# Scores of differential attention: rounded 128-row products replaced by fp32 products of 32 rows, both maps of a tile issued together

## The reference, cut to what matters

```python
q = _rope(_to_heads(q, 2 * DA_HEADS), pos).reshape(b, DA_HEADS, 2, l, DA_DQK)   # DA_DQK = 32
k = _rope(_to_heads(k, 2 * DA_HEADS), pos).reshape(b, DA_HEADS, 2, l, DA_DQK)
...
s = jnp.einsum('bhcqd,bhckd->bhcqk', qi, k).astype(jnp.float32) * scale
...
p = jax.nn.softmax(jnp.where(mask, s, NEG), axis=-1)
w = (p[:, :, 0] - lam * p[:, :, 1]).astype(v.dtype)
return jnp.einsum('bhqk,bhkv->bhqv', w, v)
```

## Time and profile before

| | us |
|---|---|
| median of 3 runs | 3943.01 (3940.19 to 3950.31) |
| the profiled execution, its own time | 3950.02 |
| its span | 3948.2 |
| PE busy | 3323.5 (84% of the span) |
| DVE busy | 1687.9 (43%) |
| ACT busy | 784.7 (20%) |
| granted TensorE clock, mean | 0.899 |

### The profile page before, as it was taken

How to read it: one execution, slowest core, us unless ns; L and a number is a source line. 1 busy time by engine, 2 the same in 40 slices (tenths; PEclk the granted TensorE clock), 3 DMA queues, 4 the chain that set the end, 5 groups by cost and what they waited for, 6 DMA issues and landing times.

```text
span 3948.2 us, 46980 instructions
## 1 busy us (share of the span) xinstructions
PE 3323.5 (84%) x15268; PEld 2148.3 (54%) x15268; DVE 1687.9 (43%) x2463; ACT 784.7 (20%) x1830; POOL 121.8 (3%) x131
## 2 busy tenths in 40 slices
PE   5999788878796599999769997888787965999994
PEld 3666556656542355555436665566666433555552
DVE  4777524443424122332267775244434241233324
ACT  2222223332211011111122222233322110111111
POOL 2100000000000100000100000000000001000001
PEclk9999997887897799999979998977888977999997
DMA  9400100000100999999820001000001008999996
GB/s 263 137 21 11 38 12 6 6 7 11 43 3 22 355 410 411 410 408 410 313 87 22 21 11 39 12 6 6 7 11 43 3 12 349 414 407 410 409 411 258
DMA packets 141079, 615.53 MB, mean 156 GB/s; under 512 B 13721, under 2 KB 48025, under 8 KB 123033
## 3 DMA queue, kind: packets, MB, share of 16 engines
q1 hardware_dynamic: 104952, 495.89, 31.9%
q0 software_dynamic: 16944, 60.89, 4.8%
q10 hardware_dynamic: 19056, 57.16, 3.9%
HBM read 538.34 MB, written 75.56 MB: 155 GB/s over the span
## 4 chain that ended last, share of the span: by engine, by line
PE 75%; DVE 7%; issue 7%; DMA 5%; ACT 3%; POOL 2%; ACTq 1%; DVEq 1%; SPq 0%; POOLq 0%
PE ps L1080 7%; PE ps L1037 7%; PE ps L1235 6%; PE ps L1336 6%; PE ps L1436 6%; PE ps L1426 6%; PE ps L1395 5%; PE ps L1172 5%; PE ps L1401 5%; PE ps L1453 3%; PE ps L1250 3%; PE ps L1300 3%; DMA arena<-xg 3%; PE ps L1135 3%; PE ps L1160 2%
## 5 line engine op out<-in xcount | busy, mean ns | idle before, releaser
L1172 PE MATMUL ps<-arena 128*64 128x128 f32 (+2 forms) x1440 | 276.3, 331 | 72.4 <-ACT arena L771 40.5
L1080 PE MATMUL ps<-arena 128*128 128x260 f32 x1024 | 294.6, 429 | 34.8 <-DVE rounded L1636 21.1
L1671 DVE TENSOR_REDUCE negmax<-ps 16x1 f32<-16x16 f32 (+8 forms) x216 | 151.5, 705 | 396.1 <-PE ps L1140 395.1
L1037 PE MATMUL ps<-arena 128*128 128x512 f32 (+1 forms) x768 | 259.7, 497 | 5.4 <-DVEq L541 3.2
L1172 PEld LDWEIGHTS ps<-arena 128*64 128x64 f32 (+1 forms) x1440 | 184.1, 163 | 146.5 <-issue 139.7
L1395 PE MATMUL ps<-arena 128*128 128x512 f32 x560 | 254.0, 607 | 2.6 <-ACT arena L959 2.6
L751 ACT ACTIVATE arena<-ps,negmax 16x16 f32<-16x16 f32 (+8 forms) x216 | 151.0, 700 | 519.0 <-DVE negmax L1671 514.8
L1235 PE MATMUL ps<-arena 128*128 128x256 f32 (+1 forms) x1152 | 251.6, 380 | 0.0
L1336 PE MATMUL ps<-arena 128*128 128x512 f32 (+1 forms) x576 | 251.6, 595 | 0.0
L1436 PE MATMUL ps<-arena 128*64 128x256 f32 x2240 | 249.5, 381 | 0.0
L1401 PE MATMUL ps<-arena 128*128 128x256 f32 x1120 | 247.4, 379 | 0.0
(11 more groups left out here) (306 smaller groups left out, 4276.2 us busy)
## 6 DMA issues: line engine op xcount, KB each, us to landing
arena<-w SPq DMA_DIRECT2D x210, 2048.0 KB, 12.9
xg<-arena POOLq DMA_DIRECT2D x51, 512.0 KB, 12.2
arena<-xg ACTq DMA_DIRECT2D x39, 512.0 KB, 10.1
xg<-arena ACTq DMA_DIRECT2D x35, 512.0 KB, 7.6
arena<-w_in SPq DMA_DIRECT2D x16, 1024.0 KB, 5.7
arena<-xg ACTq DMA_DIRECT2D x35, 256.0 KB, 11.2
xg<-arena ACTq DMA_DIRECT2D x70, 128.0 KB, 9.2
arena<-w_in SPq DMA_DIRECT2D x16, 512.0 KB, 4.3
```

Of the source, the lines that this page charges most:

```text
L1037: mm = pe.matmul(dst[0:hi - lo, a:b], w[:, k, lo:hi], uT[:, k, a:b], start=(k == 0), stop=(k == KD - 1))
L1080: mm = pe.matmul(out, w_qk[b][:, k, :], uT[:, k, lo:hi], start=(k == 0), stop=(k == KD - 1), skip_group_check=True)
L1172: mm = pe.matmul(ps[0:AW, 7, at:at + r], V[0:rows(i), i, n * AW:(n + 1) * AW], WT[0:rows(i), g % 3, m * P:m * P + r], start=(i == 0), stop ...
L1671: v.tensor_reduce(negmax[0:r, at:at + 1], flat[0:r, side:side + wide_], AX.X, ALU.max, negate=True)\
```

## The change

Pieces `c` to `f`, their table `sel`, its load and the split into high and low parts are gone. After the rotary the DVE's last addition is made as two of 64 rows, which put q (rows of both maps) and k at the same 64 partitions: `operands_of` gives for a differential head fp32 q and k of 64 rows. Scores are plain fp32 products of 32 rows: map 0 on rows 0 to 31, map 1 on rows 32 to 63. A new function writes both maps of a tile at one point, the start of the step, a product of map 0 and one of map 1 in turn; only tile 8, and the first tile of the forgetting heads, are still written unit by unit. The plans put the remaining pieces `a` and `b` of the next head into steps 8 and 0 to 3, and none into steps 4 to 7.

```diff
 PLAN_DA = {
     8: [[], [], ["a0.0@2"], ["a0.1@2"], ["a0.2@2"], ["a0.3@2"]],
...
-    1: [["c0@4"], ["a2.1@2", "b1@1"], ["d0@4"], ["a2.2@2", "e0@1"], ["f0@4"], ["a2.3@2", "c1@1"]],
...
+    0: [[], [], ["b0@4"], ["a1.0@2"], ["a1.1@2"], ["a1.2@2"]],
+    1: [["a1.3@2"], [], ["b1@4", "a2.0@2"], ["a2.1@2"], ["a2.2@2", "o@1"], ["a2.3@2"]],
+    2: [["g@1"], [], ["b2@4", "a3.0@2"], ["a3.1@2"], ["a3.2@2"], ["a3.3@2"]],
+    3: [[], ["b3@2"], [], [], [], []]}
...
         def operands_of(n):
-            return sets[(n + 1) % 2]
...
+            return (turned_sets if n < HEADS else sets)[(n + 1) % 2]
...
-                    g = "cdef".index(kind)
-                    if g == 0:
-                        pe.wait_ge(t_parts, ONE + H0 + x + 1)
-                    pe.matmul(out, sel[:, 2 * g, :], xh[(n * PARTS + x) % 2][:, 0:hi - lo], start=True, stop=False)
...
-                    pairs_ = [(ops[2 * c], ops[2 * c + 1])] if n < HEADS else \
...
+                    if n < HEADS:
+                        pairs_ = [tuple(x[DQK * c:DQK * c + DQK] for x in ops)]
...
+                def both_scores(u):
...
+                    sides = [side_of(u, j), side_of(u + 1, j)]
...
+                    if u >= 2:
+                        wait_alone(pe, t_P, ONE + U0 + u)
+                    for x, y in chunks(wide_):
+                        for m, side in enumerate(sides):
+                            pe.matmul(flat[0:r, side + x:side + y], q[DQK * m:DQK * m + DQK, cols(j)],
+                                      k[DQK * m:DQK * m + DQK, x:y], start=True, stop=False, skip_group_check=True)
+                    for side in sides:
+                        for x, y in chunks(wide_):
...
+                                mm = pe.matmul(flat[0:r, side + lo:side + y], ident_r[:, 0:r],
+                                               causal_r[:, at:at + y - lo], start=False, stop=True, skip_group_check=True)
+                        mm.then_inc(t_S, 1)
...
+                    paired = t + 1 < HEADS * T and not late
...
+                    if paired:
+                        both_scores(new[0])
+                    elif new:
                         scores(new[0])
...
-                    if not late:
+                    if not late and not paired:
                         for u in new[1:]:
                             scores(u)
...
+                    both_ = v.tensor_tensor(ops[side][:, lo:hi], raw[half, 0:hi - lo],
+                                            rot[half, 0:hi - lo], ALU.add)
```

More of the change, by code:

```diff
@@ L1142, in scores @@
                     mm.then_inc(t_S, 1)
+                def both_scores(u):
+                    n, j, c = UNITS[u]
+                    r, wide_, (q, k) = rows(j), META + P * j, operands_of(n)
+                    sides = [side_of(u, j), side_of(u + 1, j)]
+                    if j == 0:
+                        wait_alone(pe, t_turned, ONE + layer * HEADS * PARTS + (n + 1) * PARTS)
+                    for side in sides:
+                        for bank in range(side // BANK, (side + wide_ - 1) // BANK + 1):
+                            take_bank(bank)
+                            scored[bank] = u + sides.index(side)
+                    if u >= 2:
[4 more added lines that the diff above has]
+                                      k[DQK * m:DQK * m + DQK, x:y], start=True, stop=False, skip_group_check=True)
+                    for side in sides:
+                        for x, y in chunks(wide_):
+                            lo = max(x, cols(j).start)
+                            if lo < y:
+                                at = lo - cols(j).start
+                                mm = pe.matmul(flat[0:r, side + lo:side + y], ident_r[:, 0:r],
+                                               causal_r[:, at:at + y - lo], start=False, stop=True, skip_group_check=True)
+                        mm.then_inc(t_S, 1)
                 def turn_weights(t, b):
@@ L1177, in attend_pe @@
                 scored.clear()
-                scores(0)
-                scores(1)
+                both_scores(0)
                 for t in range(TILES + 2):
@@ L1579, in _ @@
             hg = Steps(v, h_v, 35)
-            ats = Steps(v, t_v, 220)
+            ats = Steps(v, t_v, 204)
             rs = Steps(v, r_v, 93)
@@ L1595, in piece_dve @@
                 kind, bank = piece[0], int(piece[-1])
-                if kind in "cde" or piece[2:4] in (".0", ".1", ".2"):
+                if piece[2:4] in (".0", ".1", ".2"):
                     return
@@ L1658, in pieces_dve @@
                 for n, piece in pieces_at(slot - 2):
-                    split_dve(layer, n, piece)
+                    turn_dve(layer, n, piece)
                 for n, piece in pieces_at(slot - 1):
@@ L1912, in _ @@
                 if stop > 2:
-                    wait_alone(v, v_t, layer * 80 + 80)
-                    v.tensor_copy(sel, sel_read).then_inc(s_clean, 1)
+                    wait_alone(v, v_t, layer * 64 + 64)
                     v.tensor_copy(ident_r, ident[:, :]).then_inc(s_clean, 1)
@@ L2207, in constants @@
     c["c_sin"] = (np.sin(ang)[n % (DQK // 2)] * scale).astype(f)
-    sel = np.zeros((P, 8, P), f)
-    for g in range(2):
-        for side, low in ((0, (0, 0, 1, 1)), (1, (0, 1, 0, 1))):
-            for m in range(P):
-                sel[side * AW + g * DQK + m % DQK, 2 * (2 * g + side) + low[m // DQK], m] = 1
-    c["c_sel"] = sel
     fx_c = np.zeros((P, 2 + HEADS), f)
```

109 lines of the change are left out of this document (43 added, 66 removed).

## The result

The changed kernel takes 4010.74 us (median of 4, 4006.37 to 4012.82) beside 3943.41 (median of 4, 3940.19 to 3950.31) for the kernel before in the same session: a ratio of 1.017, interval 1.015 to 1.019. It is 67 us slower, where 40 us faster was forecast, and lies above the forecast range, which ended at 3955. The profiled execution took 4008.9 us, its span is 4007.0.

The account below looks back on a forecast made before the run. PE's in-order stream, with its waits, was taken as the bound. Terms of -14.6, -7.2, -4.2, +11.4, -7.5 and +2 gave -20.1 us a layer, -40 for two: 3903 us, the forecast's own range 3883 to 3923, overall range 3865 to 3955.

Parts of the forecast that it names:

- The overlap: Paired scores: products on two row groups run side by side, both maps costing what one does, 1.67 ns a column.
- Rival 1: Scores of tiles 0 to 7: row groups do not overlap, 62 us for eight heads, 3965, slower; chance 0.12.
- Rival 2: Paired scores: strict order adds one record of the first chunk each step, 24 us in all, 3927; chance 0.08.
- Stage V: Stage V loses 32 selection products of 0.11 us and 4.2 us of waits: -7.5 us a layer.
- Rival 5: Waits only move: PE's 10.9 us wait for ACT's turned weights grows, 17 us a layer, 3937; chance 0.10.
- tiles 5 to 8: Steps 4 to 6, no pieces left: -5.9 us in heads 0 to 2, +3.1 in head 3, -14.6 a layer.
- tile 4 to 5: Step 3: 5.4 us instead of 6.85 in head 1, -1.4 in three heads, -4.2 a layer.
- tiles 1 to 4: Steps 0 to 2, filled with projections, bound by PE's own work: 22 us for 26.5 in head 1, -7.2 a layer.
- the turns, from tile 8 on: Turn of a head: tile 8 scored map by map, +1.8 four times; next tile 0, +1.4 three times; +11.4 a layer.
- short weight loads: Weight loads of the short last chunks, 16 and 144 columns: +2 us a layer.
- I expect it to swing between the two and take 22.5: Steps 4 to 6: clock swings between full (18.7 us) and half (24.1), so the three steps take 22.5.
- rival 3: Steps 3 to 8: clock stays low at 0.5, 50 us for eight heads, 3953, slower by a little; chance 0.13.

Follow-up runs that it names:

- the first probe: Changed kernel with blocks of useless fp32 products added at its start, each behind 24 full products; only clock and spacing compared, total time not.
- The fillers: Changed kernel plus one useless 128-row, 384-column product in steps 4 to 6 of heads 0 to 2, a second in step 4: 3979.88 us, 1.010.
- `e3_before_together`: Kernel before, with its fp32r products, both maps of a tile written at one point, piece `b2` moved to step 2: 3975.95 us, 1.008.
- `e5_rounded_32`: Changed kernel with q and k rounded to fp32r, so each score product is one record, with less precision: 3905.11 us, 0.989.
- the second probe: Changed kernel with blocks of useless products at its start, each behind 16 lone products that lower the clock first; total time not compared.

## Why the prediction was wrong

**What held.** The overlap, on which the prediction said it would fall: 2.98 us for 2.95 worked out. Rival 1 is out. Rival 2 is out too: at half clock the rule would add a record of 0.85 us to that row, and the first two records of the first probe's block, one on each row group, start 7 ns apart (38.065 and 38.072 us). By the strict order of the Trainium skill (TensorE: Matmul & The Clock Gate, Part 3, "What overlaps and what doesn't") the 96 records of the first probe would also need one record more than 20.87 us; the trace disagrees. Stage V gave -11.0 and -9.8 for -7.5 (whose terms, 3.5 and 4.2, add to 7.7). Rival 5 did not happen as put: the outputs' wait went from 10.9 to 13.4.

**Where the forecast missed.** The terms of layer 0, read between the first maxima of all four heads (a turn runs from tile 8 to tile 1 of the next head, the last one to the end of the heads):

| us | forecast | measured |
|---|---|---|
| tiles 5 to 8 | -14.6 | +14.4 |
| tile 4 to 5 | -4.2 | +6.6 |
| tiles 1 to 4 | -7.2 | 0.0 |
| the turns, from tile 8 on | +11.4 | +26.6 |
| short weight loads | +2 | not taken apart |
| stage V | -7.5 | -11.0 |

With 0.5 us ahead of the first tile 1 the heads' terms make the 48 us that these heads grew by. In tiles 1 to 4 head 1 gained 2.4 of the 4.5 forecast, and head 3 lost 3.2 for 2. The +2 for weight loads rests on no row and no run isolates it.

**The step that failed** is "I expect it to swing between the two and take 22.5", in tiles 5 to 8. In heads 0 to 2 the clock did not swing there; it was 0.50, and the three steps took 28.8 to 28.9 us, about what they took before at 0.56 (28.4 in head 1). Idle time in them fell from 5.9 to 4.0 us in head 1, busy time rose by 2.3. In head 3 they took 31.9 for 19.4, at 0.61 for 0.82. This is rival 3, which I gave 0.13. Its argument against, that PE is busier at half clock and the clock came back before, leaned on steps that held pieces of the next head, products of 128 rows. Those are what the change took out of these steps. The fillers show it the right way round: with more PE work there the clock comes back between them and 31 us come with it.

**Rival 3's price was mis-sized as well**, 50 us against the 108 between forecast and result. Three things were missing from it. First, the step's bound: from tile 6 on, at half clock, it is not exp, maximum, join, exp with a dearer S but PE's own stream, 9.8 us from tile 6 to 7, where the prediction's price at half clock is (24.1 + 1.8) / 3 = 8.6. Second, head 3, whose first maxima of tiles 5 and 8 are 12.4 us further apart than before where +3.1 was put: the whole head had a mean clock of 0.87 and now has 0.70. Third, the turn: tile 8 of head 1 to tile 1 of head 2 takes 8.6 us more for 3.2 forecast and 2 more by the rival. The half clock lasts into tile 0 of the next head, where nothing was priced at it, and map 1 of tile 8 costs 4.21 us, with the wait for its exp, 2.67, uncovered behind it.

**Where the loss comes from**, by the experiments, against the kernel before: the common place alone 27 us (`e3_before_together`). The fp32 array time at a low clock is worth up to 106, the difference to `e5_rounded_32`; that is more than the loss, since there a chunk of both maps takes one record's time where the kernel before took two. Four row groups get 46 to 48 of it back. The thin steps themselves are worth 31 (filled with nothing) to 42 (pieces spread). These overlap and don't sum to 67. The -21 of stage V and the -11 of the rest work the other way. Of the latter 3.1 us come before the first gate product, where the prediction put the missing load of `sel` at nothing; no run took them apart.

**Not settled.** Which of gaps and thin products counts for how much: the probes have no gaps, the kernel has both. In head 1 of both kernels the clock fell at the same place, behind a stretch in which PE mostly stood still (before: a wait of 2.7 us that ends at 658.88; after: 1.8 us busy of the 5.2 ahead of 652.06). What differs is what follows: now the clock is back only with the projections of the turn, about 702 us. That the longer chain of the common place is what lowers the clock in `e3_before_together` is argued; no run took it apart.

## What to carry to other kernels

Before a change empties a step of TensorE's big products, read the granted clock of that step and of a step that looks as it will look afterwards; price the step at half clock as a sum of PE's own records, not only along the chain. Where work has to be placed somewhere, place it where PE is thin. Small fp32 products on row groups should use all four groups (46 to 48 us here), and the products of two maps overlap only where they stand together (worth 55 us with two groups, 23 with four); with rounded products of 128 rows, which don't overlap, the common place cost 27.

## What the runs showed of the hardware

- Row groups of fp32 products overlap fully: 96 records of two groups in 20.87 us and 192 records of four in 20.88, for 0.43 and 0.22 us a product; full products take 0.43 a record too. Four groups thus do 192 / 48 = 4.0 times the records of full products in the same time.
- Holding and raising the clock are not the same. Two groups of 32 rows and products of 64 rows stayed at 1.00 for 20.7 and 27.6 us when they began there, and at 0.50 for 41.8 and 54.9 us when they began there (2.4 and 1.2 GHz). Four groups, outputs of 64 columns, full products and plain transposes through the identity raised it, to means of 0.90 to 0.94 over 23 to 31 us.
- A lone group of 32 rows lost the clock in an unbroken run (mean 0.55 over 50 us; 1.00 in its first 4.3 us, 0.50 in its last 41.7), with DMA busy beside it, and as well in blocks of the second probe without DMA (0.58 to 0.63, begun at full clock). The Trainium skill, TensorE: Matmul & The Clock Gate, "Why this matters for your kernels", asks for a TensorE that is kept busy continuously to have the full clock; the lone group's block and those of two groups and 64 rows behind one were, and had half clock; the measurement decides.
- The clock can cost more than the work: one or two useless products of 128 rows in thin steps made the kernel 31 us faster, needed ones spread over the same steps 42 us.
